# First attention of a two-block kernel: second half by tiles, all distance tables resident, output weights split in pieces

## Chip, cores and metric

The kernel runs on one core of one Trainium2 chip. The metric is the device time of one execution in microseconds, the median of several runs. Engines are named as in the profile: PE (TensorE matmul), PEld (its weight loads), DVE (VectorE), ACT (ScalarE), POOL (GpSimd), SP (the queue that issues most transfers).

## The reference, cut to what matters

Two transformer blocks follow one another on 512 tokens of width 1024. The change touches the first block's attention, of which this is the core:

```python
def global_gqa_attention(q, k, v):            # 8 heads, 2 key heads
    sc = jnp.einsum('bqkgd,bskd->bkgqs', qb, k) * scale
    p = jax.nn.softmax(sc, axis=-1)
    return jnp.einsum('bkgqs,bskd->bqkgd', p, v)

def dilated_mixture_attention(q, k, v):       # 8 heads; three dilated windows
    for window, dilation in ((128, 1), (512, 4), (2048, 16)):
        o, lse = dilated_window_attention(q, k, v, window, dilation, slopes)
    w = jax.nn.softmax(stack(lses)); return sum(w * stack(outs))
```

Both results, 512 columns each for every token, are normalised on their own (root mean square of 512 columns), multiplied by a gain, and multiplied by the output weights w_out (1024 x 1024); the product is added to x. Behind it come a feed-forward part, and a second block with a state-space scan, a windowed attention and 32 experts.

## The kernel before

All is float32. Matrix products with weights are made of three products of a high and a low part: a *high part* is the ACT copy of a weight unit to a rounded format (`high_part`, L1028, one instruction over 2048 columns), the *low part* is the DVE subtraction of it from the weights (`low_part`, L1869). A unit is half a slot of the ring in SBUF, 2048 columns; two high and two low parts are kept. SP's queue loads the next unit into a half when the low part of the unit there is done (L866).

**The attention.** Tokens lie in four tiles of 128. A *unit* of attention is one head and one query tile: 64 units in 32 pairs. Units 0 to 31 are the first attention (half m = 0), 32 to 63 the dilated one (m = 1), where the three windows are folded into one 128 x 512 table of distances for each head and added to the scores. `unit_of` (L373) maps a unit to half, head and tile: in both halves two heads make a pair, the tile runs inside, and the pair of heads outside, so that tile t is complete only with pair 28+t.

Every engine runs the same loop over turns q = 0 to 34 (L1157 ACT, L1470 PE, L1992 DVE), as a pipeline written out by hand. In turn q:
- PE makes the scores of units 2q and 2q+1, transposes the probabilities of pair q-1 (four each), multiplies them with the values for pair q-2, and transposes the attended rows of pair q-3.
- DVE takes the row minimum of each score (L1997 in the first half; in the second, L2003 adds the distance table and takes the minimum in one instruction), copies one transposed probability (L2010), and scales the attended rows of pair q-3 into xn (L2015, L2018).
- ACT makes the two exponentials with their row sums (L1154), copies the other transposed probability (L1165) and the attended product (L1173).
Banks of PSUM are opened in one fixed order of eight; a bank is opened when the step that frees its content eight places earlier is done.

**Distance tables.** POOL's queue loads them (L931 to L935). There are four places, two in the arena and two in spare columns of xn. Heads 0 to 3 load when the projections are done; each of heads 4 to 7 waits for the last row minimum that reads its place (score_min) before it loads.

**Output weights.** The high and low parts of the first two units of w_out are made at the ends of turns 29 and 30 (NP-3, NP-2), each in one instruction on ACT and one on DVE. The rest are made behind the norm.

**The norm "mix1"** between attention and w_out has two halves of columns for each tile. `norm_tiles` (ACT L1065, DVE L1886) makes for a tile two squares with sums, a root, a reciprocal and two scalings in place; `mixed_at` (L405) puts tiles 0 to 2 at the ends of turns 31 to 33, tile 3 behind the loop. The squares write their unused result over the spare columns (`junk1`). `norm` on PE (L1387) opens eight banks, makes 12 cover matmuls on the first (`unread`, matmuls of 128 columns whose result nobody reads; each has two records in float32), transposes tile by tile, with 5 more cover matmuls ahead of the last transpose. `norm_drains` (L1078, L1896) then writes hT_high on ACT and hT_low on DVE, and `grow` (L1505) multiplies with w_out. In turns 30, 31 and 32 PE also makes 5 cover matmuls ahead of the transposes.

The change touches `unit_of`, `mixed_at`, the dists and their loads, the three loops, and adds `high_piece`, `low_piece`, `square` and `tile_scaled`.

Of the kernel before, what the change touches and what calls it, by code (L numbers as in the profile page):

```python
# [156 lines left out]
def two_blocks(nc, consts_d, rope1_d, dist_d, h_d, inp, out):  # L157
    ctx = ExitStack()
    with ctx:
# [111 lines left out]
        dists = [dist[:, 0, :], dist[:, 1, :], carve(0, BIASW, of=spare), carve(BIASW, BIASW, of=spare)]  # L271
# [41 lines left out]
        for n, key in enumerate(ADA_PARTS):  # L313
# [9 lines left out]
        dist_in = [sem(f"dist_in{i}") for i in range(4)]  # L323
# [9 lines left out]
            "mix1": (lambda t: xn[:, t, :], XT, [(0, 512), (512, D)], junk1, lambda j: (gains[:, 1, j:j + 1], zero)),  # L333
# [10 lines left out]
        squared = steps("norm_squared", norm_keys + [("final", t, 0) for t in range(TT)])  # L344
        rooted = steps("norm_rooted", [(s, t) for s, n in NORMS.items() for t in n[1]] + [("final", t) for t in range(TT)])
# [27 lines left out]
        def unit_of(i):  # L373

            m, pair, t, par = i // (H * TT), i // (2 * TT) % (H // 2), i // 2 % TT, i % 2
            return m, 2 * pair + par if m else pair + 4 * par, t
# [28 lines left out]
        def mixed_at(q):  # L405

            t = q - (NP - 1)
            return t if 0 <= t < TT - 1 else None
# [251 lines left out]
        def part_view(part, key):  # L660

            _, width, rows, _ = UNIT_AT[key]
            return part[:, SPLIT_AT[key] % 2, 0:rows * width].rearrange("p (j n) -> p j n", n=width)

# [262 lines left out]
        def _(pool):  # L927
# [3 lines left out]
            for h in range(H):  # L931
                if h >= 4:

                    score_min.wait(pool, NU // 2 + (h // 2 - 2) * 2 * TT + 2 * (TT - 1) + h % 2)
                pool.dma_start(dists[h % 4], dist_d[h]).then_inc(dist_in[h % 4], 16)  # L935
# [82 lines left out]
        def _(act):  # L1018
# [9 lines left out]
            def high_part(*key):  # L1028
# [5 lines left out]
                high_ready.tick(s.activation(part_view(w_high, key), raw_view(key), ACT.Copy), k)  # L1034

# [109 lines left out]
            def mixed(t):  # L1145
                att.wait(act, NU // 2 - TT + t)


# [8 lines left out]
            for q in range(NP + 3):  # L1157
                if q < NP:
                    exponent(2 * q)
                if 1 <= q <= NP:  # L1160
# [4 lines left out]
                    pt_act.tick(s.activation(probsT[:, n % 4, :], bank[:, :], ACT.Copy), n)  # L1165
                if q < NP:
                    exponent(2 * q + 1)
# [6 lines left out]
                if q in (NP - 3, NP - 2):  # L1174
                    high_part("w_out", q - NP + 3)

                t = mixed_at(q)
                if t is not None:
# [1297 lines left out]
```

## Time and profile before

| what | us |
|---|---|
| median of three runs (lowest, highest) | 1552.57 (1550.52, 1554.28) |
| the profiled execution | 1553.09 |
| its span, first to last instruction | 1551.2 |
| PE busy (share of the span) | 1472.6 (95%) |
| DVE busy | 888.3 (57%) |
| ACT busy | 529.1 (34%) |
| POOL busy | 99.7 (6%) |
| mean granted TensorE clock | 0.982 |

Busy times are sums over one profiled execution. An engine's idle time costs something only where the chain of work that ended last passes through it. A granted clock of 1.00 is 2.4 GHz, of 0.50 1.2 GHz. In the timeline a line merges like instructions that follow each other; the bracket at its end tells how long the engine was idle before it and what released it.

### The profile page before, as it was taken

The page shows a single profiled execution, that of the slowest core. Times are in us where ns is not written, and L with a number is a line of the kernel's source. Part 1 is how long each engine was busy: PE and PEld are TensorE (multiplying, and loading weights), DVE is VectorE, ACT ScalarE, POOL GpSimd, SP SyncE. Part 2 cuts the span into 40 slices and gives each one's busy share as a digit, 9 for nine tenths or more (in the row PEclk, how much of TensorE's full clock was granted, in tenths as well). Part 3 has the DMA queues.
Part 4 walks back from the last instruction along what each step waited for, and adds up shares of the span by engine and source line. Part 5 has one row for each costly group of instructions (what it writes and reads, how often), then busy time and mean ns, then how long its engine had stood idle before and what let it go on. Part 6 is the DMA issues. An engine that isn't in the chain of part 4 may idle for free.

```text
span 1551.2 us, 20718 instructions
## 1 busy us (share of the span) xinstructions
PE 1472.6 (95%) x8008; PEld 1016.5 (66%) x8008; DVE 888.3 (57%) x1561; ACT 529.1 (34%) x945; POOL 99.7 (6%) x133
## 2 busy tenths in 40 slices
PE   7999998999999999999999898989999999999996
PEld 6887666888888878888887677873443444444343
DVE  4756774467777657773474676463443444344435
ACT  5455665343343332252334785221011101111112
POOL 0000000000000000001001332001010101000100
PEclk9999998999999999999999999999999999999998
DMA  8122011155454338714112011478999999999993
GB/s 262 58 79 76 9 45 52 55 177 157 128 149 123 109 123 283 252 51 132 31 55 97 29 41 64 180 310 349 363 405 409 407 406 411 398 405 403 406 416 158
DMA packets 113594, 312.58 MB, mean 202 GB/s; under 512 B 14127, under 2 KB 65743, under 8 KB 91995
## 3 DMA queue, kind: packets, MB, share of 16 engines
q1 hardware_dynamic: 109987, 303.30, 52.6%
q0 software_dynamic: 3200, 7.87, 1.6%
q8 instruction: 65, 1.06, 0.3%
q10 hardware_dynamic: 312, 0.10, 0.0%
q14 instruction: 30, 0.25, 0.0%
HBM read 311.18 MB, written 4.25 MB: 203 GB/s over the span
## 4 chain that ended last, share of the span: by engine, by line
PE 81%; DVE 7%; DMA 4%; ACT 4%; issue 3%; SPq 1%; POOL 0%; ACTq 0%; DVEq 0%; POOLq 0%
PE bank L1374 74%; PE bank L1377 7%; DMA arena<-in_w_up 3%; SPq L872 1%; DVE hTc L2376 1%; ACT weights_high L1034 1%; ACT arena L1303 0%; DVE hT L2387 0%; DVE xn L1893 0%; DVE x_res L2265 0%; DMA gains<-in_norm_g 0%; DVE xn L2264 0%; DVE arena L2446 0%; DVE ring L2202 0%; ACT hT_high L1094 0%
## 5 line engine op out<-in xcount | busy, mean ns | idle before, releaser
L1374 PE MATMUL bank<-weights_high,hT_high 128*128 128x512 f32 (+2 forms) x736 | 255.5, 386 | 7.6 <-DVE hT_low L1911 2.9
L1374 PE MATMUL bank<-weights_low,hT_high 128*128 128x512 f32 (+2 forms) x560 | 213.0, 380 | 0.0
L1873 DVE TENSOR_TENSOR weights_low<-ring,weights_high 128x2048 fp32r<-128x2048 f32 (+2 forms) x61 | 135.7, 2224 | 134.8 <-ACT weights_high L1034 133.9
L1034 ACT ACTIVATE weights_high<-ring 128x2048 fp32r<-128x2048 f32 (+2 forms) x61 | 113.4, 1859 | 189.1 <-PE bank L1374 153.8
L1374 PE MATMUL bank<-hT_high,weights_high 128*128 128x512 f32 x416 | 163.8, 394 | 0.8 <-DVE hT_low L1911 0.8
L1374 PEld LDWEIGHTS bank<-weights_high,hT_high 128*128 128x128 f32 x736 | 139.7, 190 | 34.5 <-issue 8.6
L1374 PE MATMUL bank<-hT_high,weights_low 128*128 128x512 f32 x416 | 161.9, 389 | 0.0
L1374 PE MATMUL bank<-hT_low,weights_high 128*128 128x512 f32 x416 | 161.9, 389 | 0.0
L2376 DVE TENSOR_TENSOR hTc<-bank,mod_gain 128x512 f32<-128x512 f32 x32 | 22.1, 692 | 185.7 <-PE bank L1377 185.7
L1374 PE MATMUL bank<-ring,hTc 128*64 128x512 f32 (+1 forms) x544 | 121.0, 583 | 0.0
L1374 PEld LDWEIGHTS bank<-weights_low,hT_high 128*128 128x128 f32 x560 | 106.6, 190 | 19.4 <-issue 0.2
L1374 PE MATMUL bank<-arena,hTc 128*64 128x512 f32 x480 | 106.0, 593 | 1.0 <-DMA arena<-in_w_up 1.0
L1341 ACT ACTIVATE hTc<-bank 128x512 f32<-128x512 f32 x32 | 19.1, 597 | 214.8 <-PE bank L1374 214.8
L1374 PEld LDWEIGHTS bank<-hT_high,weights_high 128*128 128x128 f32 x416 | 78.1, 188 | 20.3 <-issue 3.4
L1374 PEld LDWEIGHTS bank<-hT_high,weights_low 128*128 128x128 f32 x416 | 78.1, 188 | 16.4
L1374 PEld LDWEIGHTS bank<-hT_low,weights_high 128*128 128x128 f32 x416 | 78.1, 188 | 15.9
L1374 PEld LDWEIGHTS bank<-ring,hTc 128*64 128x64 f32 (+1 forms) x544 | 41.4, 140 | 71.1 <-issue 70.0
L1374 PE MATMUL bank<-ring,hT 128*64 128x512 f32 x256 | 70.2, 700 | 18.4 <-DVE hT L2387 18.4
L1353 ACT ACTIVATE expert_y_high<-arena 128x512 fp32r<-128x512 f32 x32 | 20.2, 631 | 191.3 <-DVE arena L2410 191.3
L1374 PE MATMUL bank<-weights_high,hT_low 128*128 128x512 f32 (+1 forms) x224 | 85.4, 381 | 0.0
L1377 PE MATMUL bank<-const,arena 128*128 128x128 f32 (+1 forms) x465 | 73.3, 286 | 12.0 <-DVE arena L1984 5.2
L1197 ACT ACTIVATE arena<-bank,convw 128x512 f32<-128x512 f32 x44 | 34.3, 779 | 145.8 <-PE bank L1374 145.8
(336 smaller groups left out, 2373.2 us busy)
## 6 DMA issues: line engine op xcount, KB each, us to landing
arena<-in_w_down SPq DMA_DIRECT2D x16, 2048.0 KB, 16.2
ring<-in_w_gate SPq DMA_DIRECT2D x32, 1024.0 KB, 13.3
ring<-in_w_up SPq DMA_DIRECT2D x32, 1024.0 KB, 15.4
ring<-in_w_down SPq DMA_DIRECT2D x16, 2048.0 KB
arena<-in_w_gate SPq DMA_DIRECT2D x30, 1024.0 KB
arena<-in_w_up SPq DMA_DIRECT2D x30, 1024.0 KB, 16.0
xn<-in_w_ada SPq DMA_DIRECT2D x48, 512.0 KB, 4.8
ring<-in_w_up SPq DMA_DIRECT2D x44, 512.0 KB, 5.2
```

Source lines behind the costliest of these rows:

```text
L872: sp.dma_start(dst, src).then_inc(more_in, 16)
L1034: high_ready.tick(s.activation(part_view(w_high, key), raw_view(key), ACT.Copy), k)
L1197: tap_mid.tick(s.activation((conv_g, conv_v)[gv][:, f % 2, :], bank[:, :], ACT.Identity, scale=convw[:, 44 + ch:45 + ch], bias=convw[:, 13 ...
L1341: s.activation(gu[:, par, :], ps[1][:, :], ACT.Copy).then_inc(gu_ready, 1)
L1353: s.activation(y_high[:, place, :], y_scaled, ACT.Copy).then_inc(y_high_ready, 1)
L1374: return nc.tensor.matmul(o, lhsT, rhs, start=start, stop=stop)
L1377: return nc.tensor.transpose(o, i, ident[0:n, 0:n])
L1873: low_ready.tick(v.tensor_tensor(part_view(w_low, key), raw_view(key), part_view(w_high, key), ALU.subtract), k)
L2376: v.tensor_tensor(xT[:, par, :, :], ps[0][:, :].rearrange("p (j n) -> p j n", j=KT), wide(mod_gain[:, 2, :], BLK), ALU.mult).then_inc(xt_s ...
```

## The change

The second half of the attention goes tile by tile: for each tile all four pairs of heads, so that tile t is complete with pair 16+4t+3. The first half keeps its order. All eight distance tables have places of their own (the four new ones over hT, which is free between the projections and this norm's drains), and all eight loads are issued in a row, without waits between them. The first two units of w_out are split in pieces: eight high pieces of 512 columns in turns 8 to 15 on ACT, sixteen low pieces of 256 columns in turns 12 to 27 on DVE. Seven of the norm's eight squares move into the turns: the first halves of tiles 0 to 3 at the ends of turns 17 to 20, the second halves of tiles 0 and 1 at the ends of turns 23 and 27, that of tile 2 at the head of turn 31; that of tile 3 comes behind the loop. One root and one reciprocal serve tiles 0 to 2. Tile 0 is scaled in turn 33, ahead of that turn's attended rows, tiles 1 and 2 behind the loop. Cover matmuls stay in turn 32 alone. The unused result of mix1's squares goes to other columns of the arena. The diff, without the reordering of the keys of the two step counters:

```diff
-        dists = [dist[:, 0, :], dist[:, 1, :], carve(0, BIASW, of=spare), carve(BIASW, BIASW, of=spare)]
+        dists = [dist[:, 0, :], dist[:, 1, :], carve(0, BIASW, of=spare), carve(BIASW, BIASW, of=spare)] + [
+            carve(n * BIASW, BIASW, of=hT_flat) for n in range(4)]
+        junk_mix1 = carve(TT * 640, D)
...
-            m, pair, t, par = i // (H * TT), i // (2 * TT) % (H // 2), i // 2 % TT, i % 2
-            return m, 2 * pair + par if m else pair + 4 * par, t
+            m, par = i // (H * TT), i % 2
+            if m:
+                return m, 2 * (i // 2 % (H // 2)) + par, i // H % TT
+            return m, i // (2 * TT) + 4 * par, i // 2 % TT
...
-        def mixed_at(q):
-
-            t = q - (NP - 1)
-            return t if 0 <= t < TT - 1 else None
+        def last_pair(t, a):
+
+            return NP // 2 + 4 * t + 3 if a else NP // 2 - TT + t
+
+        SQUARES_AT = {NP // 2 + 1 + t: (t, 0) for t in range(TT)} | {last_pair(t, 512) + 4: (t, 512) for t in range(TT - 2)}
+        PIECE = HALF // 8
+        HIGH_PIECES = {8 + n: (n // 4, n % 4 * 2 * PIECE, n % 4 * 2 * PIECE + 2 * PIECE) for n in range(8)}
+        LOW_PIECES = {12 + n: (n // 8, n % 8 * PIECE, n % 8 * PIECE + PIECE) for n in range(16)}
...
-                if h >= 4:
-
-                    score_min.wait(pool, NU // 2 + (h // 2 - 2) * 2 * TT + 2 * (TT - 1) + h % 2)
-                pool.dma_start(dists[h % 4], dist_d[h]).then_inc(dist_in[h % 4], 16)
+                pool.dma_start(dists[h], dist_d[h]).then_inc(dist_in[h], 16)
...
+            def high_piece(key, a, b):
+
+                k = SPLIT_AT[key]
+                if a == 0:
+                    act.wait_ge(unit_in[UNIT_AT[key][0]], UNIT_AT[key][-1])
+                    products(act, SPLITS[k - 2])
+                ins = s.activation(w_high[:, k % 2, a:b], raw_piece(key, a, b), ACT.Copy)
+                if b == HALF:
+                    high_ready.tick(ins, k)
...
-            def mixed(t):
-                att.wait(act, NU // 2 - TT + t)
-
+            def square(t, a):
+
+                att.wait(act, last_pair(t, a))
+                act.wait_ge(squared.sem, squared.at["mix1", t, a] - 1)
+                squared.tick(s.activation(junk_mix1[:, a:a + 512], xn[:, t, a:a + 512], ACT.Square,
+                                          accum_out=sums[:, 2 * t + a // 512:2 * t + a // 512 + 1]), ("mix1", t, a))
...
+                if q == NP - 1:
+                    square(TT - 2, 512)
...
+                if q == NP:
+                    squared.wait(act, ("mix1", TT - 2, 512))
+                    rooted.tick(root(roots[:, 0:2 * TT - 2], sums[:, 0:2 * TT - 2], 512), ("mix1", TT - 2))
...
-                if q in (NP - 3, NP - 2):
-                    high_part("w_out", q - NP + 3)
-
-                t = mixed_at(q)
-                if t is not None:
-                    norm_tiles("mix1", mixed, [t])
-            norm_tiles("mix1", mixed, [TT - 1])
+                if q in HIGH_PIECES:
+                    i, a, b = HIGH_PIECES[q]
+                    high_piece(("w_out", i), a, b)
+                if q in SQUARES_AT:
+                    square(*SQUARES_AT[q])
+            square(TT - 1, 512)
+            squared.wait(act, ("mix1", TT - 1, 512))
+            rooted.tick(root(roots[:, 2 * TT - 2:2 * TT], sums[:, 2 * TT - 2:2 * TT], 512), ("mix1", TT - 1))
...
-                        if q >= NP - 2 and n % 2 == 0:
+                        if q == NP:
...
+            def low_piece(key, a, b):
+
+                k = SPLIT_AT[key]
+                high_ready.wait(dve, k)
+                ins = v.tensor_tensor(w_low[:, k % 2, a:b], raw_piece(key, a, b), w_high[:, k % 2, a:b], ALU.subtract)
+                if b == HALF:
+                    low_ready.tick(ins, k)
...
+            def tile_scaled(t):
+
+                for a in (0, 512):
+                    n = 2 * t + a // 512
+                    normed.tick(v.tensor_scalar(xn[:, t, a:a + 512], xn[:, t, a:a + 512], rstd[:, n:n + 1], None, ALU.mult),
+                                ("mix1", t, a))
...
+                if q == NP + 1:
+                    rooted.wait(dve, ("mix1", TT - 2))
+                    link(v.reciprocal(rstd[:, 0:2 * TT - 2], roots[:, 0:2 * TT - 2]))
+                    tile_scaled(0)
...
-                    low_part("w_out", q - NP + 3)
-                t = mixed_at(q)
-                if t is not None:
-                    norm_tiles("mix1", [t])
-            norm_tiles("mix1", [TT - 1])
+                if q in LOW_PIECES:
+                    i, a, b = LOW_PIECES[q]
+                    low_piece(("w_out", i), a, b)
+            for t in range(1, TT - 1):
+                tile_scaled(t)
+            rooted.wait(dve, ("mix1", TT - 1))
+            link(v.reciprocal(rstd[:, 2 * TT - 2:2 * TT], roots[:, 2 * TT - 2:2 * TT]))
+            tile_scaled(TT - 1)
```

## Rows read from the trace of the kernel before

**Rows 1.** The chain by engine; DMA share in 40 slices, in tenths.

```profile
PE 81%; DVE 7%; DMA 4%; ACT 4%; issue 3%; SPq 1%; POOL 0%; ACTq 0%; DVEq 0%; POOLq 0%
...
DMA  8122011155454338714112011478999999999993
```

**Rows 2.** Timeline of a turn: start us, us, engine, line, what.

```profile
217.24 1.09 PE L1377 MATMUL bank<-const,arena 128*128 128x128 f32 x8
...
217.34 0.69 DVE L2003 CUSTOM_DVE_ANT_0 arena<-bank,arena 128x512 f32<-128x512 f32 x1 [0.38 <-PE bank L1374]
...
218.07 0.72 ACT L1154 ACTIVATE arena<-arena,nmin 128x512 f32<-128x512 f32 x1 [1.20 <-DVE nmin L2003]
...
218.26 1.09 PE L1374 MATMUL bank<-hTc,arena 128*64 128x128 f32 x16
...
218.57 0.69 DVE L2010 COPY hTc<-bank 128x512 f32<-128x512 f32 x1
...
219.54 1.13 PE L1374 MATMUL bank<-arena 64*128 64x512 f32 x4
...
219.65 0.17 DVE L2015 RECIPROCAL rsums<-psums 128x2 f32<-128x2 f32 x1 [0.40 <-PE bank L1377]
...
219.85 0.48 DVE L2018 TENSOR_SCALAR xn<-bank,rsums 128x64 f32<-128x64 f32 x2
...
219.98 0.26 ACT L1173 ACTIVATE arena<-bank 128x128 f32<-128x128 f32 x1
...
220.60 1.09 PE L1377 MATMUL bank<-const,arena 128*128 128x128 f32 x8
...
220.70 0.69 DVE L2003 CUSTOM_DVE_ANT_0 arena<-bank,xn 128x512 f32<-128x512 f32 x1 [0.38 <-PE bank L1374]
```

**Rows 3.** Windows: us, busy by engine, PEclk, DMA share, GB/s.

```profile
130.00:174.00 44.00, 42.86 (x364) 27.27 (x365) 32.12 (x74) 28.68 (x82) 0.00 (x0) 1.00 0.10 35
...
180.30:224.07 43.77, 43.77 (x378) 27.95 (x379) 33.23 (x105) 28.14 (x78) 2.16 (x4) 1.00 0.13 43
...
239.50:241.80 2.30, 2.10 (x8) 1.43 (x8) 0.90 (x4) 2.30 (x7) 0.00 (x0) 0.50 0.88 353
```

**Rows 4.** Timeline of the two long turns.

```profile
226.86 1.91 ACT L1034 ACTIVATE weights_high<-ring 128x2048 fp32r<-128x2048 f32 x1
...
228.80 2.29 DVE L1873 TENSOR_TENSOR weights_low<-ring,weights_high 128x2048 fp32r<-128x2048 f32 x1 [1.75 <-ACT weights_high L1034]
...
231.01 0.68 DVE L2003 CUSTOM_DVE_ANT_0 arena<-bank,xn 128x512 f32<-128x512 f32 x1
...
237.94 0.68 DVE L2003 CUSTOM_DVE_ANT_0 arena<-bank,xn 128x512 f32<-128x512 f32 x1
```

**Rows 5.** Timeline of the tail.

```profile
239.54 1.11 PE L1377 MATMUL bank<-const,arena 128*128 128x128 f32 x4 [2.63 <-ACT arena L1154]
...
240.73 0.62 ACT L1072 ACTIVATE xn<-xn 128x512 f32<-128x512 f32 x1
...
242.07 1.28 ACT L1026 ACT_TABLE_LOAD   x1
...
252.28 0.48 DVE L2018 TENSOR_SCALAR xn<-bank,rsums 128x64 f32<-128x64 f32 x2
...
253.16 3.70 PE L1377 MATMUL bank<-const,xn 128*128 128x128 f32 x31 [1.69 <-DVE xn L2018]
...
256.22 5.47 ACT L1094 ACTIVATE hT_high<-bank,const,gains 128x512 fp32r<-128x512 f32 x8 [1.77 <-PE bank L1377]
```

**Rows 6.** Distance tables: KB each and us to landing; and POOL's first issues.

```profile
arena<-distances POOLq DMA_DIRECT2D x4, 448.0 KB, 4.2
...
127.40 1.31 POOL L935 DMA_DIRECT2D arena<-distances  x2 [126.47 <-PE bank L1374]
```

**Rows 7.** DVE forms: shape, count | busy us, mean ns | idle before.

```profile
L1873 DVE TENSOR_TENSOR weights_low<-ring,weights_high 128x2048 fp32r<-128x2048 f32 x45 | 103.1, 2292 | 64.4 <-ACT weights_high L1034 63.6
...
L1977 DVE TENSOR_TENSOR xn<-arena 128x256 f32<-128x256 f32 x8 | 3.0, 418 | 0.0
```

More of the change, by code:

```diff
@@ L322, in two_blocks @@
         x_in, const_in, more_in, ctx_in = [sem(f"x_in{t}") for t in range(TT)], sem("const_in"), sem("more_in"), sem("ctx_in")
-        dist_in = [sem(f"dist_in{i}") for i in range(4)]
+        dist_in = [sem(f"dist_in{h}") for h in range(H)]
         unit_in = {p: sem(f"unit_in_{p}") for p in ("slot0", "slot1", "slot2", "half0", "half1")}
@@ L332, in two_blocks @@
             "norm1": (lambda t: x[:, t, :], XT, [(0, D)], xn[:, 0, :], lambda j: (gains[:, 0, j:j + 1], zero)),
-            "mix1": (lambda t: xn[:, t, :], XT, [(0, 512), (512, D)], junk1, lambda j: (gains[:, 1, j:j + 1], zero)),
+            "mix1": (lambda t: xn[:, t, :], XT, [(0, 512), (512, D)], junk_mix1, lambda j: (gains[:, 1, j:j + 1], zero)),
             "norm2": (lambda t: x[:, t, :], XT, [(0, D)], junk1, lambda j: (gains[:, 2, j:j + 1], zero)),
@@ L343, in two_blocks @@
         norm_keys = [(s, t, a) for s, (_, tiles, parts, _, _) in NORMS.items() for t in tiles for a, _ in parts]
-        squared = steps("norm_squared", norm_keys + [("final", t, 0) for t in range(TT)])
-        rooted = steps("norm_rooted", [(s, t) for s, n in NORMS.items() for t in n[1]] + [("final", t) for t in range(TT)])
+        squared = steps("norm_squared", sorted(norm_keys, key=lambda k: (list(NORMS).index(k[0]), k[0] == "mix1" and k[2])) +
+                        [("final", t, 0) for t in range(TT)])
+        rooted = steps("norm_rooted", [(s, t) for s, n in NORMS.items() for t in n[1] if s != "mix1" or t >= TT - 2] +
+                       [("final", t) for t in range(TT)])
         normed = steps("normed", [k for k in norm_keys if k[0] != "norm1"])
@@ L663, in part_view, with raw_piece @@
             return part[:, SPLIT_AT[key] % 2, 0:rows * width].rearrange("p (j n) -> p j n", n=width)
+        def raw_piece(key, a, b):
+            at = PLACES[UNIT_AT[key][0]][0]
+            return ring_flat[:, at + a:at + b]
         def raw_view(key):
@@ L1999, in _ @@
                             _, h, t = unit_of(i)
-                            dve.wait_ge(dist_in[h % 4], 16 * (h // 4 + 1))
+                            dve.wait_ge(dist_in[h], 16)
                             banks.filled(dve, ("probsT", i - 4))
                             a = (TT - 1 - t) * P
-                            score_min.tick(v.tensor_tensor_reduce(probs[:, i % 4, :], bank[:, :], dists[h % 4][:, a:a + T],
+                            score_min.tick(v.tensor_tensor_reduce(probs[:, i % 4, :], bank[:, :], dists[h][:, a:a + T],
                                                                   1.0, 3e38, ALU.add, ALU.min, nmin[:, i:i + 1]), i)
@@ L2020, in _ @@
                     att.tick(ins, p)
-                if q in (NP - 3, NP - 2):
-                    low_part("w_out", q - NP + 3)
-                t = mixed_at(q)
-                if t is not None:
-                    norm_tiles("mix1", [t])
-            norm_tiles("mix1", [TT - 1])
+                if q in LOW_PIECES:
[6 more added lines that the diff above has]
+            tile_scaled(TT - 1)
             norm_drains("mix1")
```

## The prediction

> **What bounds the kernel now.** I read the chain of work that ended last first: 81% of it is PE, 7% DVE, 4% ACT [rows 1]. So time comes off where PE stands still, not where another engine gets less to do. The edits touch one stage, the first attention (127 to 253 us) and the norm "mix1" behind it, so I then read the timeline of one of its 32 turns. A turn on PE is eight transpose records (217.24 to 218.26, 1.02 us), sixteen attended records and one transposition of the attended rows (to 219.54, 1.28 us) and four score records (to 220.60, 1.06 us), and the next turn starts at once: 3.36 us, all of it PE [rows 2]. The others wait: DVE is idle 0.40 and 0.38 us in a turn, ACT 1.20 us in one place, just ahead of its first exponential, waiting for DVE's row minimum [rows 2]. The stretch from 180.30 to 224.07 us holds thirteen such turns, 3.37 us each, with PE busy all of it; in the first half PE is busy 42.86 of 44.00 us, and ACT 28.68, which leaves ACT about 1.2 us in a turn there too [rows 3].
>
> Then two turns break it. In turn 29 ACT makes the high part of an output weight unit in one instruction of 1.91 us behind its attended copy, DVE stands 1.75 us waiting for it, takes 2.29 us for the low part, and only then comes to the next row minimum, at 231.01 instead of 227.43. Turn 30 does the same, and its successor starts at 237.94 [rows 4]. Two regular turns would have ended at 230.79. So 7.15 us are lost.
>
> The tail is the third thing. PE waited 2.63 us for the exponential at 239.54, and its granted clock, 1.00 in the turns of the second half, reads 0.50 (1.2 instead of 2.4 GHz) behind that wait [rows 3, 5]. Three tiles of the norm follow inside the last turns, each with two squares, a root and two scalings that wait for one another across ACT and DVE; the first root also loads a table (1.28 us) [rows 5]. The last attended rows are scaled at 252.76, which frees the last of the eight banks that the norm's transposes open, so the transposes start at 253.16 and the first drain of hT at 256.22. From the minimum of 237.94 to that drain are 18.28 us.
>
> **The change, part by part.**
>
> *Tile-major second half.* The same 32 units in another order, so no instruction is added. Tile t is finished with pair 16+4t+3 instead of 28+t. It needs all eight distance tables from turn 16 to 19 on, so they all load at once: POOL's queue issues four in 2.4 us from 127.40, and a table lands 4.2 us (448 KB) from its issue [rows 6]. Eight are 3.7 MB, and at the 4.2 us of one table each, with no overlap at all, the last would land 34 us later, at 161. First use is at 180.3. Cost nothing; the cover is 19 us. What stood behind their waits on POOL's queue is not needed before stage two.
>
> *Weight pieces.* Taken out: two ACT instructions of 1.91 us and two DVE instructions of 2.29 us, and with them the stall of 7.15 us. Put in: eight high pieces of 512 columns on ACT in turns 8 to 15, and sixteen low pieces of 256 columns on DVE in turns 12 to 27. No trace row shows these forms. For the high piece the nearest row is the 512-column square from SBUF, 0.62 us [rows 5]; it goes into ACT's idle, 1.20 us in the second half and of that size in the first. For the low piece the nearest row is the subtraction-like TENSOR_TENSOR of 256 columns, 0.42 us; an eighth of 2.29 (0.29) bounds it from below, half of a full part (1.15) from above; I take 0.42 [rows 7]. It stands directly ahead of the row minimum, where DVE is idle 0.38, with 0.78 in the whole turn. Consecutive records overlap (two minima of 0.69 take 1.23, from 217.34 to the copy at 218.57 [rows 2]), so about 0.35 of it counts: the minimum moves by 0 to 0.05 us. What does a later minimum cost? It starts at 217.34, its exponential at 218.07, and the second one is done when ACT's attended copy starts at 219.98; PE's transposes of the next turn begin at 220.60 and reach the second unit at 221.1. That is about 1 us of slack, so PE sees nothing. Cost taken: 0.
>
> The Trainium skill speaks against this part: "VectorE: DVE Perf Modes", section "The TRN2 errata", says that each instruction with an SBUF source pays a fixed extra latency, and advises operands of at least 512 elements. The rows agree on the fixed cost (0.42 against 0.29 for an eighth). By that page the sixteen pieces are about 2.2 us more DVE work than two whole parts, which is lost only if DVE bounds the turn.
>
> *Squares ahead.* Six of the eight squares of the norm go into turns 17 to 20, 23 and 27, and one into turn 31, at about 0.7 us each with the read of the accumulator (the 0.62 of its row and the read, overlapped) into ACT's 1.20 of idle. None reloads a table: the square at 240.73 ran right behind an exponential, and the load came only with the root [rows 5]. The square of turn 31 waits for pair 27, scaled at about 230.4, and is over before that turn's first exponential at 231.5. Cost 0. Only the last half of tile 3 is squared behind the last pair.
>
> *One root for three tiles, and later scalings.* The table load stays (1.28), ahead of ACT's copy of pair 30. Tile 0 is scaled ahead of pair 30's rows on DVE, tiles 1 and 2 behind pair 31, beside ACT's last square and root.
>
> *Cover matmuls.* Ten records each leave turns 30 and 31, where PE waited; with the wait gone they would only cost.
>
> **The sum for the tail.** Without the stall the minimum of turn 31 is at 230.79. PE ends its scores at 230.69. Two transposes, pair 29, the transposition of 28: to 233.0. Ten cover records at the transposes' 0.119 (3.70 us for 31 [rows 5]): to 234.2; probability 62 is ready at about 232.4. Transposes 62 and 63: 235.2. Pair 30: 236.5. Pair 31, whose last copy on DVE ends at 235.9: 237.5. Transpositions of 30 and 31 with ACT's copy (0.26) between: 238.2. Then PE has its 24 cover records, 2.9 us at the same rate: 241.1. DVE meanwhile scales tile 0 until 238.3, pair 30 until 239.0, pair 31 until 239.7, tiles 1 and 2 until 241.5, and tile 3 (ACT's square and root done at 241.0) until 242.6. So banks and tiles are there before PE needs them, the transposes start at 241.1, and the first drain follows as before 3.06 us later (256.22 less 253.16), at 244.1. Before it was at 256.22: the gain is 12.1 us, 7.15 from the two turns and 4.9 from the tail. What is late next is PE's own row of cover matmuls.
>
> The stages behind it move forward whole: their weights' loads wait for semaphores of the compute, and the DMA row is at 0 to 4 tenths in the 18th to 25th of its 40 slices, so nothing runs ahead that could take the gain back; its eleven full slices (29th to 39th) come behind that [rows 1]. The profiled execution took 1553.09 us around its span of 1551.2; less 12.1 it would be 1541.0. The median of the runs shown is 0.5 below it, so the forecast is 1552.6 less 12.1, **1540.5 us**.
>
> **The rivals.**
>
> *The clock still falls* (between). The last turns are chains across three engines, and PE has short pauses between groups. If the granted clock reads 0.5 from turn 32 to the transposes, PE's parts cost twice there: transposes 62 and 63 +1.0, pairs 30 and 31 +2.3, half of the cover records +1.3, in sum 4.6 less what waits hide (about 1). That gives 1544.1. For it: the trace shows half clock in this place [rows 3]. Against it: there it followed a wait of 2.6 us, and none over 0.4 is left in my sum. The Trainium skill's "TensorE: Matmul & The Clock Gate", section "A second HAM failure mode", tells of clocks that fall from frequent small pauses alone. By it this rival would be the likelier; the turns here, with 1.00 granted, don't show it.
>
> *The slack isn't there* (slower). The turn is really set by minimum, exponential and transpose in series, and whatever stands ahead of a minimum or an exponential lengthens it. Then sixteen low pieces cost 6.7 us (0.42), eight high pieces 5.0 (0.62) and six squares 4.2 (0.7), together 15.9, and the time is 1556.4. It decides from the point where a piece pushes the second exponential past the 1 us that I counted. For it: ACT waits for DVE and DVE for PE in every turn. Against it: PE has no idle in the turn, and cannot be late and full.
>
> *Nothing arrives at the end* (same). A later stage waits for a transfer that doesn't start earlier, and gives all of it back: 1552.6. For it: the DMA engines are full in eleven slices ahead of the end. Against it: they start full only when the compute lets them.
>
> **How the numbers follow.** Forecast 0.75; clock 0.12; nothing arrives 0.04; slack missing 0.04; other mixtures, mostly still faster, 0.05. The range takes in the forecast with its unknown terms (a low piece between 0.29 and 1.15, the chain in the tail by 1 to 2 us either way, runs that differ by 2 us) and the clock rival: 1537.0 to 1545.0. A measurement here tells about 0.2%, 3 us, from no change. Faster 0.93, same 0.04, slower 0.03.
>
> **What would show it.** Row minima of the second half every 3.36 us through turn 31, the last at about 231; no wait of PE over 0.5 us from there to the drains; granted clock 1.00 throughout; cover records that end at about 241, and the first drain of hT at about 244. Turns of 3.7 us or more with a low piece in them would make me wrong in the second rival's direction; a clock of 0.5 behind 233 in the first's; a first drain at 244 and an unchanged end in the third's.

## The result, and the profile after

Measured: 1540.65 us median (1538.76 to 1541.35, four runs) against 1552.68 (1550.52 to 1554.28, four runs). The ratio is 0.9926, 95% interval 0.9914 to 0.9938: 12.0 us faster. The forecast was 1540.5 with 1537 to 1545.

The head of the changed kernel's profile: span, and the chain that ended last.

```profile
span 1538.5 us, 20723 instructions
...
PE 83%; DVE 6%; DMA 4%; ACT 3%; issue 2%; SPq 2%; POOL 0%; DVEq 0%; POOLq 0%; ACTq 0%
```

PE's part of the chain went from 81% to 83% [rows 1], which fits a change that takes out time in which PE only waited.

The end of turn 27 and the start of turn 28 in after, with a square of the norm and a low piece between them. Columns: start us, us, engine, line, what.

```profile
220.18 0.48 DVE L2068 TENSOR_SCALAR xn<-bank,rsums 128x64 f32<-128x64 f32 x2
...
220.31 0.26 ACT L1203 ACTIVATE arena<-bank 128x128 f32<-128x128 f32 x1
220.47 0.62 ACT L1171 ACTIVATE arena<-xn 128x512 f32<-128x512 f32 x1
220.58 0.41 DVE L1910 TENSOR_TENSOR weights_low<-ring,weights_high 128x256 fp32r<-128x256 f32 x1
...
220.94 1.09 PE L1408 MATMUL bank<-const,arena 128*128 128x128 f32 x8
...
221.04 0.69 DVE L2049 CUSTOM_DVE_ANT_0 arena<-bank,arena 128x512 f32<-128x512 f32 x1
...
221.77 0.72 ACT L1179 ACTIVATE arena<-arena,nmin 128x512 f32<-128x512 f32 x1 [0.59 <-DVE nmin L2049]
```

The square (0.62) and the low piece (0.41) stand where before had idle time [rows 2]. The minimum starts at 221.04, 0.10 behind PE's transposes, exactly as before [rows 2]; ACT's idle is 0.59 instead of 1.20. All turns of the second half take 3.36 or 3.37 us, through turn 31; the two long ones [rows 4] are gone. The prediction took the costs of the two new forms from their nearest rows. These are their own rows in after, grouped by shape (shape, count | busy us, mean ns | idle before). The low pieces on DVE:

```profile
L1910 DVE TENSOR_TENSOR weights_low<-ring,weights_high 128x256 fp32r<-128x256 f32 x16 | 6.6, 415 | 0.0
```

and on ACT the high pieces and the squares of attended rows:

```profile
L1054 ACT ACTIVATE weights_high<-ring 128x512 fp32r<-128x512 f32 x8 | 5.2, 645 | 0.0
L1171 ACT ACTIVATE arena<-xn 128x512 f32<-128x512 f32 x8 | 5.0, 625 | 1.7 <-DVE xn L2068 1.6
```

The tail of after, from the row minimum of turn 31 to the first drain, to compare with [rows 5]:

```profile
231.13 0.69 DVE L2049 CUSTOM_DVE_ANT_0 arena<-bank,hT 128x512 f32<-128x512 f32 x1 [0.37 <-PE bank L1405]
...
233.24 1.28 PE L1405 MATMUL bank<-const 128*128 128x128 f32 x10
...
234.36 0.60 PE L1408 MATMUL bank<-const,arena 128*128 128x128 f32 x4
...
234.80 1.28 PE L1405 MATMUL bank<-const 128*128 128x128 f32 x10
...
235.61 1.28 ACT L1038 ACT_TABLE_LOAD   x1
...
236.91 0.30 ACT L1038 ACTIVATE roots<-sums,const 128x6 f32<-128x6 f32 x1
...
239.42 2.84 PE L1405 MATMUL bank<-const 128*128 128x128 f32 x24
...
240.21 0.48 DVE L2068 TENSOR_SCALAR xn<-bank,rsums 128x64 f32<-128x64 f32 x2
...
240.72 0.63 ACT L1171 ACTIVATE arena<-xn 128x512 f32<-128x512 f32 x1 [1.58 <-DVE xn L2068]
...
242.10 3.59 PE L1408 MATMUL bank<-const,xn 128*128 128x128 f32 x31
...
242.38 0.88 DVE L2035 TENSOR_SCALAR xn<-xn,rstd 128x512 f32<-128x512 f32 x2
245.06 5.47 ACT L1116 ACTIVATE hT_high<-bank,const,gains 128x512 fp32r<-128x512 f32 x8 [3.28 <-PE bank L1408]
```

Three windows of after over it and the turns ahead (columns as in [rows 3]): PEclk stays at 1.00, and PE is busy 6.70 of 6.70, 7.60 of 7.60 and 6.19 of 6.40 us. The longest wait of the matmul queue in the tail is 0.2 us. The cover records (matmuls whose result nobody reads) stand there as twice ten in turn 32 (233.24, 234.80) and 24 ahead of the norm's transposes (239.42).

```profile
224.40:231.10 6.70, 6.70 (x59) 4.27 (x60) 5.11 (x16) 4.64 (x13) 0.00 (x0) 1.00 0.12 46
231.10:238.70 7.60, 7.60 (x86) 6.68 (x86) 4.04 (x14) 5.04 (x12) 0.00 (x0) 1.00 0.00 0
238.70:245.10 6.40, 6.19 (x58) 5.98 (x55) 4.46 (x15) 1.34 (x5) 0.00 (x0) 1.00 0.01 3
```

The DMA issues of the distance tables in after, to compare with [rows 6] (KB each, median us to landing):

```profile
hT<-distances POOLq DMA_DIRECT2D x4, 448.0 KB, 8.3
arena<-distances POOLq DMA_DIRECT2D x2, 448.0 KB, 4.1
xn<-distances POOLq DMA_DIRECT2D x2, 448.0 KB, 6.5
```

Eight in a row take longer, up to twice as long for the ones over hT (8.3 instead of 4.2). They are issued by 132.2 and so land by about 141; DVE first reads a table over hT at 187.39, over 40 us later.

In what follows, times of the stage are counted from POOL's issue of the first table, which lies at the start of the attention: 127.40 us in before, 127.73 in after. (The 0.33 between them is from ahead of the change.) "Last row minimum" is the first of the two minima of turn 31, the last turn that has any. So counted, it came at 110.5 before and at 103.4 after, and the first drain of hT at 128.8 and 117.3: 11.5 us earlier. Two of SP's loads behind the stage show how this travels. The first loads of w_up, in before:

```profile
274.28 35.93 SPq L866 DMA_DIRECT2D ring<-in_w_up  x6
```

and in after:

```profile
263.15 35.92 SPq L881 DMA_DIRECT2D ring<-in_w_up  x6
```

The load of w_gate for the second slot of the first experts, in before:

```profile
1004.19 0.33 SPq L786 DMA_DIRECT2D ring<-in_w_gate  x1
```

and in after:

```profile
991.75 0.33 SPq L801 DMA_DIRECT2D ring<-in_w_gate  x1
```

11.1 us at the first load of w_up (11.5 with the later start), 12.4 at the first weights of the experts' second slot. The 1.3 us between can't be put down to the change: from the one load to the other the profiled executions took 729.9 us in before and 728.6 in after, and in the twelve kernels below, which are all alike there, 725.5 to 729.6. That spread of 4 us behind the stage is also why the stage's own times are used below beside the medians. Where PE doesn't wait they repeat to 0.01 us (the last minimum at 103.39 or 103.40 in eight kernels, the drain at 117.33 in three); of a tail with waits there is one profiled execution for each kernel.

### The profile page after: what moved, and what is told of

Same layout as the page of the kernel before. It is cut to its first block, busy times and chain, and to the rows that moved or that the text cites. A ratio compares the mean times of both kernels' runs of the same rounds, so it can differ in the third digit from the quotient of the medians.

```text
span 1538.5 us, 20723 instructions
## 1 busy us (share of the span) xinstructions
PE 1464.0 (95%) x7998; PEld 1011.3 (66%) x7998; DVE 888.9 (58%) x1573; ACT 529.4 (34%) x949; POOL 99.5 (6%) x133
## 4 chain that ended last, share of the span: by engine, by line
PE 83%; DVE 6%; DMA 4%; ACT 3%; issue 2%; SPq 2%; POOL 0%; DVEq 0%; POOLq 0%; ACTq 0%
PE bank L1405 75%; PE bank L1408 7%; DMA arena<-in_w_up 3%; SPq L887 1%; DVE hTc L2428 1%; ACT arena L1334 0%; SPq L884 0%; DVE hT L2439 0%; DVE ring L2254 0%; DVE x_res L2317 0%; DVE xn L2316 0%; DVE arena L2498 0%; ACT hT_high L1116 0%; ACT early_up L1319 0%; ACT weights_high L1046 0%
## 5 line engine op out<-in xcount | busy, mean ns | idle before, releaser
L1904 DVE TENSOR_TENSOR weights_low<-ring,weights_high 128x2048 fp32r<-128x2048 f32 (+2 forms) x59 | 131.1, 2222 | 131.0 <-ACT weights_high L1046 130.1
L1046 ACT ACTIVATE weights_high<-ring 128x2048 fp32r<-128x2048 f32 (+2 forms) x59 | 109.6, 1858 | 189.3 <-PE bank L1405 154.5
L1405 PE MATMUL bank<-ring,hT 128*64 128x512 f32 x256 | 68.6, 686 | 18.3 <-DVE hT L2439 18.3
L1405 PEld LDWEIGHTS bank<-arena,hTc 128*64 128x64 f32 x480 | 34.6, 137 | 70.8 <-issue 70.5
## 6 DMA issues: line engine op xcount, KB each, us to landing
ring<-in_w_gate SPq DMA_DIRECT2D x32, 1024.0 KB, 12.3
```

Of the source, the lines that this page charges most:

```text
L1405: return nc.tensor.matmul(o, lhsT, rhs, start=start, stop=stop)
L1904: low_ready.tick(v.tensor_tensor(part_view(w_low, key), raw_view(key), part_view(w_high, key), ALU.subtract), k)
```

## The experiments

The theory: every us of the gain comes from PE's waits in turns 29 to 32 and in the norm's chain, the regular turns have about 1 us of slack that hides all pieces, and PE's own cover matmuls are late next. The rivals are with each run. "Issue" is POOL's first issue of a table.

| kernel | last row minimum behind the issue | first drain | median us (lowest to highest, runs) | before beside it | ratio to before (95%) |
|---|---|---|---|---|---|
| before | 110.5 | 128.8 | 1552.68 (1550.5 to 1554.3, 4) |  |  |
| changed | 103.4 | 117.3 | 1540.65 (1538.8 to 1541.4, 4) | 1552.68 | 0.9926 (0.9914 to 0.9938) |
| order and tables alone | 110.5 | 130.3 | 1551.87 (1549.4 to 1554.1, 10) | 1551.79 | 0.9996 (0.9984 to 1.0008) |
| before with the pieces alone | 104.6 | 124.1 | 1547.54 (1544.4 to 1550.9, 10) | 1551.84 | 0.9973 (0.9961 to 0.9986) |
| changed, parts whole in turns 29, 30 | 110.5 | 122.9 | 1544.77 (1542.5 to 1546.7, 6) | 1551.79 | 0.9950 (0.9934 to 0.9966) |
| changed, norm late | 103.4 | 123.4 | 1545.66 (1543.3 to 1549.1, 10) | 1551.79 | 0.9959 (0.9947 to 0.9970) |
| changed, roots by tile | 103.4 | 117.3 | 1538.38 (1) | 1551.84 |  |
| changed, 5 cover matmuls in turn 32 | 103.4 | 116.2 | 1540.50 (1535.8 to 1541.2, 4) | 1551.79 | 0.9926 (0.9904 to 0.9949) |
| changed, low pieces of 1024 | 103.4 | 117.3 | 1542.03 (1) | 1551.24 |  |
| changed, low parts whole in 18, 22 | 105.2 | 119.1 | 1542.84 (1) | 1551.24 |  |
| changed, high and low parts whole | 105.2 | 119.1 | 1540.61 (1) | 1551.84 |  |
| changed, cover 5 and 6 | 103.4 | 115.1 | 1536.62 (1535.8 to 1541.5, 6) | 1551.24 | 0.9907 (0.9889 to 0.9925) |
| changed, cover 0 and 6 | 103.4 | 114.4 | 1536.80 (1534.5 to 1538.6, 5) | 1551.24 | 0.9900 (0.9882 to 0.9918) |
| changed, cover 0 and 6, low pieces of 1024 | 103.4 | 114.4 | 1537.94 (1536.0 to 1540.5, 6) | 1551.84 | 0.9909 (0.9891 to 0.9926) |

The kernels were timed in groups, each with runs of the kernel before beside it; its median differs between the groups by 1.4 us (1551.24 to 1552.68). So a median is compared with the one beside it, and two medians of different groups tell differences of 1 to 2 us badly. The single runs have no interval.

**One part alone: order and tables.**

```diff
+            if m:
+                return m, 2 * (i // 2 % (H // 2)) + par, i // H % TT
...
+                pool.dma_start(dists[h], dist_d[h]).then_inc(dist_in[h], 16)
```

> The kernel before with the tile-major second half and the eight resident distance tables alone; weight parts whole in turns 29 and 30, norm and cover matmuls as before. My theory (the order is free and brings nothing by itself): 1552.7 us, row minima of the second half every 3.36 us up to turn 29, first drain of hT 0 to 0.3 us from that of before. Rival (the tables arrive late or disturb turns 16 to 19): a wait of DVE for a table in those turns, and some us more. Rival (the order itself carries part of the gain): 2 us or more faster.

The ratio to before is 0.9996 (0.9984 to 1.0008), every turn is as before: the order is free and brings nothing by itself. One thing was not expected: the drain came 1.5 us later than in before, where at most 0.3 was expected. (The profiled execution was the longest of the ten, 1554.06 us with a median of 1551.87, so this may not be so in all of them.) PE's rows of this kernel in the norm, and two windows of it:

```profile
248.38 2.84 PE L1375 MATMUL bank<-const 128*128 128x128 f32 x24
253.29 5.32 PE L1378 MATMUL bank<-const,xn 128*128 128x128 f32 x31 [2.06 <-DVE xn L2019]
```

```profile
246.00:252.00 6.00, 4.14 (x42) 3.61 (x39) 2.44 (x11) 3.42 (x11) 0.00 (x0) 1.00 0.01 3
253.70:256.70 3.00, 3.00 (x16) 3.00 (x15) 1.05 (x3) 1.00 (x5) 0.00 (x0) 0.50 0.00 0
```

The transposes took 5.32 us instead of 3.70 [rows 5]. The granted clock was back at 1.00 here from 246 to 252 and reads 0.50 again from 253.7, behind pauses of 1 to 2 us; in before it was at 0.50 from about 239 to 249 and back by the transposes. Both are tails with waits, made of the same instructions; where in them the half clock fell is the difference of 1.5 us between these two executions.

**One part alone: the pieces, on the kernel before.**

```diff
-                if q in (NP - 3, NP - 2):
-                    high_part("w_out", q - NP + 3)
+                if q in HIGH_PIECES:
+                    high_piece(("w_out", i), a, b)
...
-                    low_part("w_out", q - NP + 3)
+                if q in LOW_PIECES:
+                    low_piece(("w_out", i), a, b)
```

> The kernel before with the pieces alone: eight high pieces in turns 8 to 15, sixteen low pieces in turns 12 to 27; order, tables, norm and cover matmuls as before. My theory: the 7.1 us of the two turns go, less 1.1 us for the cover records of turn 30, which now stand in PE's way: last row minimum at 104.5 us behind the first table's issue; the tail is the long one of the late norm, 20 us, so the first drain is at 124.5 and the time 1548 us. Rival (the pieces bring their 7.1 whole): drain at 121.7, 1545 us.

Last minimum 104.6, drain 124.1, 1547.54 us, ratio 0.9973 (0.9961 to 0.9986). As the theory said: turn 30 took 4.53 instead of 3.36, its ten cover records being PE work now that PE doesn't wait. So those records had to go together with the stall. The tail behind the last minimum grew too, from 18.3 to 19.5 us: the scaled rows of pair 28, with which the norm's chain begins, start 3.67 us behind that minimum instead of 2.02, since in before PE had done all of turn 31's work, cover included, while DVE was held. The pieces alone are worth 4.7 us of the stage.

**One part undone: the weight parts whole in turns 29 and 30.**

```diff
-                if q in HIGH_PIECES:
-                    high_piece(("w_out", i), a, b)
+                if q in (NP - 3, NP - 2):
+                    high_part("w_out", q - NP + 3)
...
-                if q in LOW_PIECES:
-                    low_piece(("w_out", i), a, b)
+                    low_part("w_out", q - NP + 3)
```

> The changed kernel with the two high and two low parts whole again in turns 29 and 30, all else as changed. My theory: each of the two turns takes 6.9 instead of 3.36 us again, 7.1 us in sum, and PE waits over 2 us in both and meets half clock behind them, which costs 1 to 3 us more: 1549 to 1551 us. Rival (the squares ahead and the shorter tail can absorb the stall): 1541 to 1544.

I missed this one: 1544.77 us, where 1549 to 1551 was expected, and 7.0 below the before beside it. Its timeline of turns 29 to 31 and of the norm's transposes:

```profile
227.54 1.90 ACT L1046 ACTIVATE weights_high<-ring 128x2048 fp32r<-128x2048 f32 x1
...
229.48 2.29 DVE L1903 TENSOR_TENSOR weights_low<-ring,weights_high 128x2048 fp32r<-128x2048 f32 x1 [1.74 <-ACT weights_high L1046]
...
231.69 0.68 DVE L2048 CUSTOM_DVE_ANT_0 arena<-bank,hT 128x512 f32<-128x512 f32 x1
...
233.38 2.27 PE L1407 MATMUL bank<-const,arena 128*128 128x128 f32 x8 [1.93 <-ACT arena L1179]
...
237.30 1.28 PE L1404 MATMUL bank<-const 128*128 128x128 f32 x10
238.62 0.68 DVE L2048 CUSTOM_DVE_ANT_0 arena<-bank,hT 128x512 f32<-128x512 f32 x1
...
240.22 0.65 PE L1407 MATMUL bank<-const,arena 128*128 128x128 f32 x4 [1.64 <-ACT arena L1179]
...
248.01 3.57 PE L1407 MATMUL bank<-const,xn 128*128 128x128 f32 x31
...
250.96 2.79 ACT L1116 ACTIVATE hT_high<-bank,const,gains 128x512 fp32r<-128x512 f32 x4 [3.27 <-PE bank L1407]
```

and three windows of it:

```profile
231.00:233.30 2.30, 0.45 (x4) 0.00 (x0) 2.30 (x6) 0.88 (x3) 0.00 (x0) 1.00 0.39 61
233.38:235.60 2.22, 2.12 (x10) 1.41 (x10) 0.77 (x4) 2.22 (x5) 0.00 (x0) 0.50 0.89 354
238.70:243.00 4.30, 2.79 (x30) 2.62 (x32) 2.91 (x10) 3.64 (x8) 0.00 (x0) 1.00 0.70 244
```

The turns are 6.94 and 6.93 us, as expected, and PE waits 1.93 us until 233.38; its next eight transposes take 2.27 us instead of 1.09, at a granted clock of 0.50. But from the last minimum (238.62) to the drain are 12.3 us instead of 13.9. While DVE is held for the second time, until 238.6, PE finishes what lies ahead of unit 62's transposes, half clock and all, and the ten cover records ahead of them too (237.30). So these transposes start 1.60 us behind the last minimum (240.22), as soon as the exponential is there; in the changed kernel, where PE still has that work and that cover to do, they start 3.23 us behind it (234.36 less 231.13). That is the 1.6 us, and so the stall costs 5.55 us of the stage, not 7.1. The half clock costs nothing: it was over by 237, and PE then waited 1.64 us with the clock back at 1.00. My expectation missed both terms: how much of PE's work fits into the stall, and that the half clock lies inside it.

**One part undone: the norm late.**

```diff
-                if q in SQUARES_AT:
-                    square(*SQUARES_AT[q])
-            square(TT - 1, 512)
...
+                t = mixed_at(q)
+                if t is not None:
+                    norm_tiles("mix1", mixed, [t])
+            norm_tiles("mix1", mixed, [TT - 1])
```

> The changed kernel with the norm's squares, roots and scalings where they were before (tiles 0 to 2 in turns 31 to 33, tile 3 behind the loop). My theory: three tiles of the chain attended rows, two squares, root, scalings follow one another at about 3.4 us each, the last attended rows come at about 246 instead of 240.7, the first drain 4 to 5 us later: 1545 us. Rival (PE's cover matmuls bind the tail anyway): at most 1 us slower than the changed kernel, 1541 to 1542.

1545.66 us, 6.1 below the before beside it where the changed kernel was 12.0 below; the drain is 6.0 later, where 4 to 5 was expected. The transposes start at 118.7 behind the issue instead of 114.4: 4.35 us are the chain of attended rows, two squares, root and scalings, which takes 3.4 us for each tile. The rest, 1.7, is the half clock, which fell on the transposes here (5.29 us for the 31).

**The norm ahead, but with a root for each tile.**

```diff
-                if q == NP:
-                    squared.wait(act, ("mix1", TT - 2, 512))
...
+                if NP - 1 <= q < NP + 2:
+                    t = q - NP + 1
+                    squared.wait(act, ("mix1", t, 512))
+                    rooted.tick(root(roots[:, 2 * t:2 * t + 2], sums[:, 2 * t:2 * t + 2], 512), ("mix1", t))
...
```

> The changed kernel with a root, a reciprocal and two scalings for each of tiles 0, 1 and 2 at the ends of turns 31, 32 and 33; the squares stay ahead. My theory (what counted was that no square waits for attended rows any more): the first drain within 0.5 us of the changed kernel's 117.3 behind the first table's issue. Rival (the single root for three tiles is part of the gain): 1 us or more later.

The drain is at 117.33, the same to 0.01. With this much cover on PE the single root is worth nothing; the squares ahead are what counts. (With less cover it wasn't run.)

**The slack of a turn.** Low parts in four pieces of 1024 columns:

```diff
-        LOW_PIECES = {12 + n: (n // 8, n % 8 * PIECE, n % 8 * PIECE + PIECE) for n in range(16)}
+        LOW_PIECES = {16 + 3 * n: (n // 2, n % 2 * 4 * PIECE, n % 2 * 4 * PIECE + 4 * PIECE) for n in range(4)}
```

> The changed kernel with the low parts in four pieces of 1024 columns (turns 16, 19, 22, 25) instead of sixteen of 256. A piece (1.2 us) is longer than DVE's idle ahead of the row minimum (0.38), so the minimum comes about 0.8 us later. My theory (about 1 us of slack between minimum and PE's transposes): PE's turns stay at 3.36 us, the last row minimum 103.4 us behind the first table's issue as in the changed kernel. Rival (no slack, what stands ahead of a minimum lengthens the turn): each of the four turns 0.8 us longer, the last minimum at 106.6.

The minimum behind a piece came 0.68 us late (a turn of 4.04, then one of 2.69), and PE lost nothing: last minimum 103.40, drain 117.33. Whole low parts at the ends of turns 18 and 22:

```diff
+        LOW_PIECES = {18 + 4 * n: (n, 0, HALF) for n in range(2)}
```

> The changed kernel with each low part in one instruction (2.29 us) at the ends of turns 18 and 22; high pieces stay. The minimum comes 1.8 us late. My theory (slack of about 1 us): PE loses 0.7 to 0.9 us in each of the two turns, the last row minimum at 104.9 to 105.2 us behind the first table's issue. Rival (no slack): 1.8 us each, at 107.1.

Its timeline behind the first whole part:

```profile
190.15 2.28 DVE L1910 TENSOR_TENSOR weights_low<-ring,weights_high 128x2048 fp32r<-128x2048 f32 x1
...
192.34 0.68 DVE L2049 CUSTOM_DVE_ANT_0 arena<-bank,hT 128x512 f32<-128x512 f32 x1
...
193.07 0.72 ACT L1179 ACTIVATE arena<-arena,nmin 128x512 f32<-128x512 f32 x1 [2.32 <-DVE nmin L2049]
...
194.03 0.63 PE L1408 MATMUL bank<-const,arena 128*128 128x128 f32 x4
```

The minimum came at 192.34 instead of 190.60, the transposes at 194.03. The last minimum is at 105.17, 1.77 us later for two parts: 0.88 each, of 1.74 us that the minimum was late. So the slack is 0.86 us.

And with the high parts whole too, in turns 9 and 13:

```diff
+        HIGH_PIECES = {9 + 4 * n: (n, 0, HALF) for n in range(2)}
+        LOW_PIECES = {18 + 4 * n: (n, 0, HALF) for n in range(2)}
```

> The changed kernel with nothing split at all: each high part in one ACT instruction (1.91 us, turns 9 and 13), each low part in one DVE instruction (2.29 us, turns 18 and 22), never one waiting for the other. My theory (the old stall came from high and low part in series behind one another in one turn; the high part alone stays within the slack, the low part exceeds it by 0.9): the last row minimum at 105.2 us behind the first table's issue, as with whole low parts alone, 1.8 us over the changed kernel. Rival (whole parts are what costs, wherever they are): 108 to 110.5, as before the change.

105.17 and 119.09, as with whole low parts alone. Nothing is split here, and 5.4 of the 7.1 us stay gained. So size alone doesn't make the stall. What is different in it is that high and low part stand one behind the other in one turn: DVE waits 1.75 us for the high part, then takes 2.29 for the low one, and the minimum comes 3.58 us late [rows 4] instead of 1.74. (The parts also stand in earlier turns here; both parts in one turn, but early, wasn't run.)

**What is late next: PE's cover matmuls.** In turn 32 ahead of unit 62's transposes alone:

```diff
-                        if q == NP:
+                        if q == NP and n % 2 == 0:
                             unread(bank, 5)
```

> The changed kernel with the cover matmuls of turn 32 ahead of one unit's transposes alone (10 records instead of 20). This is what my sum had reckoned with. My theory (PE is late next, so its records count one for one): 10 records at 0.12, the first drain 1.0 to 1.2 us earlier than in the changed kernel, 1539.5 us. Rival (DVE's scalings or ACT's table load are late next): the drain moves by under 0.3 us.

The drain is 1.12 us earlier (116.21), as expected. The medians don't tell the two kernels apart (ratio to before 0.9926 for both). Then 6 instead of 12 ahead of the norm's transposes as well:

```diff
-            UNREAD = {"mix1": (12, 5), ...
+            UNREAD = {"mix1": (6, 5), ...
```

> The changed kernel with 5 cover matmuls in turn 32 (instead of 10) and 6 instead of 12 ahead of the norm's transposes. My theory (PE's cover records are late next): the first drain comes 1.1 us earlier from the first and about 1.0 from the second, at 115.2 us behind the first table's issue (117.3 in the changed kernel, 116.2 with the first alone); granted clock stays 1.00; 1538.5 us. Rival (the clock falls with less cover): 0.50 in the stretch of the transposes, no gain or a loss of 1 to 2 us.

The drain at 115.13, clock 1.00 throughout, 1536.62 us, ratio 0.9907 (0.9889 to 0.9925). And none in turn 32:

```diff
-                        if q == NP:
-                            unread(bank, 5)
...
+            UNREAD = {"mix1": (6, 5), ...
```

> The changed kernel with no cover matmuls in turn 32 and 6 ahead of the norm's transposes. PE then waits under 1 us for the exponentials of turn 31. My theory: the chain of ACT's copies, table load and root binds behind it, so the first drain comes 0.3 to 0.9 us earlier than with 5 in turn 32, at 114.3 to 114.9 us behind the first table's issue, clock 1.00; 1538 us. Rival (the clock needs the cover): 0.50 behind turn 32, 1540 or more.

PE's rows of it in the tail, and a window over the whole of it:

```profile
232.67 0.77 PE L1408 MATMUL bank<-const,arena 128*128 128x128 f32 x5
233.60 0.63 PE L1408 MATMUL bank<-const,arena 128*128 128x128 f32 x4 [0.17 <-ACT arena L1179]
...
237.14 1.50 PE L1405 MATMUL bank<-const 128*128 128x128 f32 x12
238.66 3.69 PE L1408 MATMUL bank<-const,xn 128*128 128x128 f32 x31
```

```profile
230.00:243.00 13.00, 12.61 (x123) 10.48 (x120) 9.26 (x31) 7.95 (x21) 0.00 (x0) 1.00 0.01 1
```

The drain is at 114.39, 2.9 us ahead of the changed kernel; PE waits 0.17 us for an exponential, and the clock reads 1.00 over the whole tail. 1536.80 us, ratio 0.9900 (0.9882 to 0.9918). Put together with the 1024-column pieces:

```diff
-                        if q == NP:
-                            unread(bank, 5)
...
+        LOW_PIECES = {16 + 3 * n: (n // 2, n % 2 * 4 * PIECE, n % 2 * 4 * PIECE + 4 * PIECE) for n in range(4)}
...
+            UNREAD = {"mix1": (6, 5), ...
```

> The changed kernel with what the runs have shown put together: low parts in four pieces of 1024 columns, no cover matmuls in turn 32, 6 ahead of the norm's transposes. My theory: the first drain as without cover in turn 32, at 114.4 us behind the first table's issue, clock 1.00, 1537 us, 3 to 4 us faster than the changed kernel. Rival (late minima and thin cover together cost again): 116 or more.

114.38, 1537.94 us, ratio 0.9909 (0.9891 to 0.9926), no more than without the larger pieces. These last three kernels are 13.9 to 14.6 us below the before beside them, the changed one 12.0; by their stage they are 2.2 to 2.9 us ahead of it. Their intervals overlap that of the changed kernel, so it is the stage that shows the gain.

## Why the prediction was right, step by step

- **The regular turns.** Cost 0 for all pieces and squares: right. A low piece took 0.415 us (0.42 taken), a high piece 0.645 (0.62 taken), and the minimum moved by less than 0.01 us. The slack that this rested on was read as about 1 us and came out as 0.86. A piece takes 0.42 us against 0.29 for an eighth of a whole part, so splitting adds work to DVE; it cost the kernel nothing, since PE bounds the turn. The Trainium skill advises at least 512 elements because each instruction with an SBUF source pays a fixed extra latency ("VectorE: DVE Perf Modes", section "The TRN2 errata"). The trace agrees on the fixed cost, as the 0.42 shows, and the pieces below that size cost the kernel no time here. The splitting was finer than needed.
- **The two long turns.** 7.15 us forecast, 7.14 measured in the row minima. But as the worth of the pieces it is too much: undone alone they cost 5.55 us of the stage, and added alone they bring 4.7. The step that had this wrong is the one that counted the turns and the tail as two separate sums. PE does 1.6 us of the tail's work while the stall lasts, which is lost to the tail when the stall goes. The total was built along PE's new path and so didn't suffer.
- **The tail.** 4.9 us forecast, 4.35 measured: 13.93 us from the last minimum to the drain, where my sum had 13.3. The term of the sum that was mis-sized is the cover in turn 32: I read its new condition as ten records, and it makes twenty, ten ahead of each unit. Ten of them cost 1.12 us, as the run with 5 shows. Three small terms went the other way: up to the 24 cover records PE was 0.24 us faster than summed (8.29 less 1.12, against 7.41), the 24 took 2.68 us instead of 2.9 (239.42 to 242.10), and the rest to the drain 2.96 instead of 3.0. In sum 0.62 more than forecast. That PE's cover matmuls would be late next was right.
- **The number.** 1540.5 forecast and 1540.65 measured is closer than the sum was. The stage gave 11.5 us where 12.1 were forecast, and the stretch behind it, which varies by 4 us by itself, took 1.3 us less in the one profiled execution of after than in that of before. That these fit together to 0.15 us is luck; that the stage came within 0.6 us is not.
- **Which part brings what.** Norm late costs 6.0 us, 1.7 of them from where the half clock fell; weight parts whole cost 5.55; before, which has both, the old order and the old cover, is 11.5 behind. The order by itself brings 0 by its medians. It is only what lets the squares go ahead, since a tile is complete earlier with it.
- **The stages behind.** The gain arrives whole: 11.5 us at the drain, 12.4 at the experts, where the 1.3 us from the first load of w_up on lie inside what those stages vary by from one execution to the next.
- **The clock rival.** It didn't happen in the changed kernel, nor with 12 instead of 44 cover records from turn 32 to the norm's transposes, where PE waits up to 0.2 us in several places and the clock reads 1.00. Where parts were undone the half clock came back behind waits of 1 us and more, and its price was 0 to 1.7 us by where it fell. The Trainium skill tells of a kernel with bf16 matmuls of 512 columns whose clock went up and down from frequent small pauses ("TensorE: Matmul & The Clock Gate", section "A second HAM failure mode"). These tails, with float32 records of 128 columns and pauses of up to 0.2 us, kept 1.00 and don't show it.
- **The slower rival** is excluded: a row minimum that is 0.68 us late costs nothing (low pieces of 1024).

Open: the tails with waits were each read from a single profiled execution, so whether the half clock falls at the same place in every execution of a kernel wasn't shown; nor is it shown why it stayed away at some of the waits.

## What to carry to other kernels

Where one engine is full in every turn of a pipeline, count how late another may deliver before the full one notices, and put extra work anywhere within that slack; measured once (here by one piece that is too long), it tells how finely to split. Here four pieces of 1024 columns did as well as sixteen of 256, and a whole part cost 0.88 us. What hurt most was two dependent pieces on two engines, one behind the other in one turn. Cover matmuls that were free inside a wait become work as soon as the wait is gone: recount them with every change that removes one.

## What the runs showed of the hardware

- The place at which the granted clock reads 0.50 in a tail with waits of 1 to 2.6 us differed even between two executions whose tails are the same instructions (before, and the order alone). By where it fell it moved the end of the stage by 0 to 1.7 us (31 transposes: 3.70 us in before, 5.32 and 5.29 in two of the runs).
- PE kept a granted clock of 1.00 through the whole tail with waits of up to 0.2 us and with 12 instead of 44 cover records from turn 32 to the norm's transposes.
- The stretch of 730 us behind the stage, the same program in all kernels, varied by 4 us between executions (725.5 to 729.9).
